# Hybrid encoder step: per-layer embeddings' products from float32 to split operands, in a new place of the queues

## The reference

```
z   = rmsnorm(h) @ w_in                      # split into latents, gates g_a, g_c, convolution input
y_a = rmsnorm(attention * silu(g_a))         # 512 columns, after the attention
y_c = rmsnorm(silu(layernorm(conv)) * silu(g_c))   # 512 columns
h   = h + concat([y_a, y_c]) @ w_out
gate = sigmoid(rmsnorm(h) @ w_pg)
h   = h + gate * (p @ w_pe)                  # p: per-layer input embeddings, 256 wide
```

## Time and profile before

| | us |
|---|---|
| median of three runs | 765.39 |
| the profiled execution's own time | 765.02 |
| its span | 762.9 |
| TensorE busy | 749.0 |
| VectorE busy | 562.0 |
| ScalarE busy | 428.2 |
| GpSimd busy | 91.6 |

### The profile page before, as it was taken

One profiled execution on the slowest core, in us unless ns is written; L12 is line 12 of the kernel. 1 busy time (PEld: TensorE's weight loads), 2 busy tenths in 40 slices (PEclk: granted clock), 3 DMA queues, 4 the chain that ended last, 5 costly groups with the idle time before them and its releaser, 6 DMA issues.

```text
span 762.9 us, 10602 instructions
## 1 busy us (share of the span) xinstructions
PE 749.0 (98%) x3749; PEld 601.8 (79%) x3749; DVE 562.0 (74%) x1084; ACT 428.2 (56%) x996; POOL 91.6 (12%) x161
## 2 busy tenths in 40 slices
PE   9999999999999999999999999999999999999995
PEld 7899887767777588888888988877678767888874
DVE  3459978979877986546453798988888879655577
ACT  3865655665566733263366575647655758223564
POOL 1500323420001400000000020353000000000000
PEclk9999999999999999999999999999999999999998
DMA  8742222410011343412282223233111014332203
GB/s 271 229 128 83 88 73 86 115 36 15 35 35 28 123 167 130 134 56 83 66 279 77 91 76 85 82 81 83 41 36 43 1 54 154 110 125 74 88 5 138
DMA packets 50681, 70.69 MB, mean 93 GB/s; under 512 B 15582, under 2 KB 28154, under 8 KB 50614
## 3 DMA queue, kind: packets, MB, share of 16 engines
q1 hardware_dynamic: 44746, 59.27, 24.6%
q0 software_dynamic: 5824, 10.73, 5.2%
q10 hardware_dynamic: 60, 0.02, 0.0%
HBM read 60.79 MB, written 9.27 MB: 92 GB/s over the span
## 4 chain that ended last, share of the span: by engine, by line
PE 89%; DVE 6%; ACT 2%; DMA 1%; issue 1%; SPq 0%; POOL 0%; ACTq 0%
PE acc L692 20%; PE acc L701 20%; PE acc L698 19%; PE sharedT L616 5%; PE acc L836 5%; PE sharedS L930 4%; PE sharedO L944 4%; PE sharedO L616 2%; PE sharedS L616 2%; DVE VT L1623 2%; PE sharedT L902 1%; PE sharedS L888 1%; PE sharedO L874 1%; PE sharedS L889 1%; PE sharedO L913 1%
## 5 line engine op out<-in xcount | busy, mean ns | idle before, releaser
L692 PE MATMUL acc<-WHI,XHI 128*128 128x512 f32 (+1 forms) x710 | 304.7, 429 | 0.8 <-ACT WHI L1115 0.5
L701 PE MATMUL acc<-WHI,XLO 128*128 128x512 f32 (+1 forms) x710 | 274.7, 387 | 0.0
L698 PE MATMUL acc<-WLO,XHI 128*128 128x512 f32 (+1 forms) x710 | 274.3, 386 | 0.0
L1623 DVE SCALAR_TENSOR_TENSOR VT<-UX,CWT,VT 128x640 f32<-128x640 f32 x240 | 211.5, 883 | 5.0
L692 PEld LDWEIGHTS acc<-WHI,XHI 128*128 128x128 f32 x710 | 133.7, 188 | 29.8 <-issue 6.2
L1553 DVE SCALAR_TENSOR_TENSOR WLO<-WR,GT,WHI 128x512 fp32r<-128x512 f32 (+1 forms) x142 | 98.7, 737 | 78.8 <-ACT WHI L1115 78.6
L698 PEld LDWEIGHTS acc<-WLO,XHI 128*128 128x128 f32 x710 | 133.9, 189 | 27.3 <-issue 6.2
L701 PEld LDWEIGHTS acc<-WHI,XLO 128*128 128x128 f32 x710 | 133.3, 188 | 26.2
L1115 ACT ACTIVATE WHI<-WR,GT 128x512 fp32r<-128x512 f32 (+1 forms) x142 | 93.4, 708 | 85.5 <-PE acc L701 85.3
L1336 ACT ACTIVATE SB<-SB,NBIAS 128x128 f32<-128x128 f32 (+2 forms) x80 | 44.4, 555 | 37.0 <-DVE NBIAS L1682 35.6
L1115 ACT ACTIVATE PT<-sharedT 128x384 f32<-128x384 f32 (+1 forms) x80 | 35.6, 444 | 37.1 <-PE sharedT L616 36.9
(11 more groups left out here) (213 smaller groups left out, 884.4 us busy)
## 6 DMA issues: line engine op xcount, KB each, us to landing
WR<-in_w_in_dram SPq DMA_DIRECT2D x32, 256.0 KB, 3.1
WR<-in_w_in_dram SPq DMA_DIRECT2D x16, 512.0 KB, 3.7
WR<-in_w_out_dram SPq DMA_DIRECT2D x16, 512.0 KB, 3.7
WR<-in_w_pg_dram SPq DMA_DIRECT2D x16, 512.0 KB, 3.5
H<-in_x_prompt_dram SPq DMA_DIRECT2D x16, 256.0 KB, 5.2
WR<-in_w_in_dram SPq DMA_DIRECT2D x8, 416.0 KB, 5.8
residual_spill<-H SPq DMA_DIRECT2D x5, 512.0 KB, 3.4
H<-residual_spill SPq DMA_DIRECT2D x10, 256.0 KB, 3.4
```

The costliest lines, as they stand in the source:

```text
L692: mm(out, hi, w_hi, start=(first and k == 0), stop=False)
L698: mm(out, hi, w_lo, start=False, stop=False)
L701: last = mm(out, lo, w_hi, start=False, stop=(final and k == 1))
L1623: stt(out=out, in0=src, scalar=w, in1=out, op0=ALU.mult, op1=ALU.add).then_inc(conv_done, 1)
```

## The change

The embeddings' products become quanta like all others. Their weight pieces are parts and get split (without a gain column); PTR is copied to XHI (rows 4 and 5, free after gc's third piece) by ScalarE in unit 22, and GpSimd subtracts to make XLO. The block pe1 moves behind oa0. The y tiles are transposed two tiles earlier against the embeddings' products. VectorE starts on y ahead of the convolution's norm, and gates and normalisations of the convolution are dealt out between the residual additions. Three taps move. Numbers of parts behind these rise by one or two throughout.

```diff
-BLOCKS = [... "cv", "pe0", "pe1", "oa0", "oa1", "oc0", "oc1", "pg0", "pg1"]
+BLOCKS = [... "cv", "pe0", "oa0", "pe1", "oa1", "oc0", "oc1", "pg0", "pg1"]
-PARTS = [c for c in CHUNKS if c[1][:2] != "pe"]
+PARTS = CHUNKS
-TAP["turn"] = _take(1)
-for _u, _m in enumerate((2, 1, 0, 4, 1, 1, 4, 2, 1, 2, 0, 2, 1, 1, 4, 2, 1, 2, 0, 2, 1, 1, 4, 1, 0, 1, 1, 3)):
+TAP["turn"] = _take(2)
+for _u, _m in enumerate((1, 1, 1, 3, 1, 1, 4, 2, 1, 2, 0, 2, 1, 1, 4, 2, 1, 2, 0, 2, 1, 1, 4, 1, 1, 1, 1, 2)):
...
# SP, piece(j)
-                    if before in PART:
-                        sp.wait_ge(split_ready, PART[before] + 1)
-                    else:
-                        sp.wait_ge(acc_filled[TILES - 1], BLK[pl, name] + 1)
+                    sp.wait_ge(split_ready, PART[before] + 1)
...
# TensorE
-            copied_wait(pe, (l, "p2"))
-            embed(0, 0)
+            pe.wait_ge(p_low, 2 * (l + 1))
+            quantum("pe0", 0, 0)
             values(UNITS - 1)
-            for t in range(1, TILES):
-                embed(0, t)
-            embed(1, 0)
             for t in range(1, TILES):
-                embed(1, t)
-                turn_ya(t - 1)
+                quantum("pe0", 0, t)
+                if t > 1:
+                    turn_ya(t - 2)
             for c in range(2):
                 for t in range(TILES):
                     copied_wait(pe, (l, ("y", t, 0)))
                     quantum("oa0", c, t)
-                    if (c, t) == (0, 0):
-                        turn_ya(TILES - 1)
+                    if c == 0 and t < 2:
+                        turn_ya(t + 3)
+            for t in range(TILES):
+                quantum("pe1", 0, t)
...
# ScalarE
+            def embeddings_high():
+                part_used(act, PART[l, "gc", 2])
+                for k in range(2):
+                    copy(XHI[:, :, 4 + k, :], PTR[:, k, :].rearrange("p (t e) -> p t e", e=P)).then_inc(p_high, 1)
+                if u == 22:
+                    embeddings_high()
+                if u in (28, 30):
+                    high(first_i + 20 + (u - 28) // 2)
...
             for t in range(TILES):
+                embedding_out(1, t)
+                if t == 0:
+                    high(first_i + 24)
                 if t == 1:
+                    v_tanh_out(4)
             for t in range(TILES):
                 act.wait_ge(yc_ready, TILES * l + t + 1)
                 mean_square(Y[:, t, 512:1024], 20 + t, 512)
+            high(first_i + 25)
...
# VectorE
+                if u >= 30:
+                    low(first_i + u - 10)
...
             sample_heads_out()
-            norm_of_conv()
             head_out(HEADS - 1)
...
             low_half((l, ("y", 0, 0)))
+            norm_of_conv()
+            low_half((l, ("y", 1, 0)))
+            low_half((l, ("y", 2, 0)))
+            norm_of_conv_end()
+            low(first_i + 22)
+            low_half((l, ("y", 3, 0)))
+            normed(0)
+            low_half((l, ("y", 4, 0)))
+            normed(1)
             conv_gate(0)
+            normed(2)
             norm_of_y(0)
+            low(first_i + 23)
             for t in range(TILES):
                 onto_residual("oa0", t)
+                if t in (1, 2):
+                    conv_gate(t)
+                    normed(t + 2)
+            low(first_i + 24)
+            conv_gate(3)
+            conv_gate(4)
+            low(first_i + 25)
             norm_of_y(1)
...
# GpSimd
+            for k in range(2):
+                pool.wait_ge(p_high, 2 * l + k + 1)
+                nc.gpsimd.tensor_tensor(XLO[:, :, 4 + k, :], PTR[:, k, :].rearrange("p (t e) -> p t e", e=P),
+                                        XHI[:, :, 4 + k, :].bitcast(F32), ALU.subtract).then_inc(p_low, 1)
```

More of the change, by code:

```diff
@@ L36 @@
 MAGIC = float(0x5F3759DF)
-BLOCKS = ["u0", "zA", "u1", "ga", "gc", "cv", "pe0", "pe1", "oa0", "oa1", "oc0", "oc1", "pg0", "pg1"]
+BLOCKS = ["u0", "zA", "u1", "ga", "gc", "cv", "pe0", "oa0", "pe1", "oa1", "oc0", "oc1", "pg0", "pg1"]
 BLK = {(l, name): l * len(BLOCKS) + i for l in range(DEPTH) for i, name in enumerate(BLOCKS)}
@@ L311, in build @@
         p_in = sem("p_in")
+        p_high = sem("p_high")
+        p_low = sem("p_low")
         wq_rot = sem("wq_rot")
@@ L431, in first_rows, with first_x @@
             return 2 if name[:2] == "oc" else 0
+        def first_x(name):
+            return 2 if name[:2] == "pe" else first_rows(name)
         def gain_column(i, k):
             l, name, c = PARTS[i]
+            if name[:2] == "pe":
+                return None
             col = G_IN if name in ZCOL else G_OUT if name[0] == "o" else G_PG
@@ L680, in quantum @@
                 for k in ks:
-                    row = 2 * (c + first_rows(name)) + k
+                    row = 2 * (c + first_x(name)) + k
                     hi, lo = XHI[:, t, row, :], XLO[:, t, row, :]
@@ L826, in filler @@
                     quantum(name, c, t, (k,))
[L828 to L839, removed]
             def turn_conv(t):
@@ L1445, in scalar_layer, with ya_square @@
             act.wait_ge(conv_done, CONVS * (l + 1))
[L1446 to L1451, removed]
+            def ya_square(t):
                 act.wait_ge(ya_ready, TILES * l + t + 1)
                 mean_square(Y[:, t, 0:512], 15 + t, 512)
-                if t == 1:
[L1455 to L1463, removed]
+            embedding_out(0, 0)
+            embedding_out(0, 1)
+            ya_square(0)
+            embedding_out(0, 2)
+            high_half((l, ("y", 0, 0)))
+            ya_square(1)
+            embedding_out(0, 3)
+            high_half((l, ("y", 1, 0)))
+            embedding_out(0, 4)
+            high_half((l, ("y", 2, 0)))
+            high(first_i + 22)
+            high_half((l, ("y", 3, 0)))
+            ya_square(2)
+            high_half((l, ("y", 4, 0)))
+            ya_square(3)
+            ya_square(4)
+            v_tanh_out(0)
+            v_tanh_out(1)
+            high(first_i + 23)
+            v_tanh_out(2)
+            v_tanh_out(3)
+            for t in range(TILES):
+                embedding_out(1, t)
+                if t == 0:
+                    high(first_i + 24)
+                if t == 1:
+                    v_tanh_out(4)
             for t in range(TILES):
@@ L1471, in scalar_layer @@
                 if t == 0:
-                    high(first_i + 24)
-            for i in range(25, 28):
+                    high(first_i + 26)
+            for i in range(27, 30):
                 high(first_i + i)
@@ L1857, in vector_layer @@
                 if t == 0:
-                    low(first_i + 24)
+                    low(first_i + 26)
                 if t > 1:
@@ L1862, in vector_layer @@
             onto_residual("oa1", 4)
-            low(first_i + 25)
-            low(first_i + 26)
+            low(first_i + 27)
+            low(first_i + 28)
             for t in range(TILES):
@@ L1867, in vector_layer @@
                 if t == 3:
-                    low(first_i + 27)
+                    low(first_i + 29)
                 if t > 1:
@@ L1872, in vector_layer @@
             low_half((l, ("h", 4, 0)))
-            low(first_i + 28)
+            low(first_i + 30)
             for t in range(TILES):
@@ L1878, in vector_layer @@
                 if t == 1:
-                    low(first_i + 29)
-            low(first_i + 30)
-            low(first_i + 31)
+                    low(first_i + 31)
+            low(first_i + 32)
+            low(first_i + 33)
             dve.wait_ge(squares, SQUARES * l + 30)
@@ L1884, in vector_layer @@
             nc.vector.tensor_scalar(HR[:, 0:5], RS[:, 25:30], 0.5, None, ALU.mult).then_inc(rstd_ready, 1)
-            low(first_i + 32)
+            low(first_i + 34)
             def gate_embedding(half, t):
@@ L1900, in vector_layer @@
             if last:
-                low(first_i + 35)
+                low(first_i + 37)
                 dve.wait_ge(lnf_in, 16)
@@ L1907, in vector_layer @@
             else:
-                low(first_i + 34)
-                low(first_i + 35)
+                low(first_i + 36)
+                low(first_i + 37)
                 gains(l + 1)
@@ L1912, in vector_layer @@
                     low_half((l + 1, ("x", t, 0)))
-                low(first_i + 36)
+                low(first_i + 38)
             def rstd_of_tile(t):
```

45 lines of the change are left out of this document (16 added, 29 removed).

## The result

The changed kernel takes 768.63 us (median of six runs, 767.65 to 770.47). The kernel before took 765.24 beside it (six runs, 764.79 to 766.03). The ratio is 1.0048, with an interval of 1.0036 to 1.006: slower by half a per cent. The profiled execution took 770.33 us, one of the longest, with a span of 768.4.

The account below looks back on a forecast made before the run. The prediction took TensorE's queue, busy 98% of the span, as the bound. Its terms, -3.6 - 1.7 + 5.3 + 1.5, gave +1.5 us a layer, +3.0 in all, hence 768.4 us, with a range of 764.2 to 770.8.

Parts of the forecast that it names:

- A, products: Embeddings' products on TensorE: ten tiles as split products, 1.36 us each in place of 1.72, save 3.6 us a layer.
- B, taps: Convolution taps dealt anew: TensorE's stalls before the scores of units 6 and 30 go, gaining 1.7 us a layer.
- C, hold: Unit 22: GpSimd's two subtractions hold up VectorE's taps, costing 1.5 us a layer (bounds 0 and 2.7).
- D, VectorE late: Behind the units: VectorE can't keep up and TensorE stalls, costing 5.3 us a layer (bounds 4.3 and 6.3).
- the replay: Step-by-step timing of the new order from the first embeddings product: five TensorE stalls, 5.3 us a layer.
- Rival 4: TensorE's clock falls in the new stalls: half speed for 3 us costs 1.5 a layer more, 771.4; chance 0.03.
- Rival 2: VectorE's additions come in time, stalls behind the units halve to 2.7 us, no GpSimd hold: 760.1 us; chance 0.08.

Follow-up runs that it names:

- the new dealing alone: The kernel before with only the new deal of the convolution's taps: 761.44 us, ratio 0.9948.
- the one with zeros: The changed kernel with GpSimd writing zeros into the embeddings' low part in place of subtracting: 766.63 us, ratio 1.0012.
- the late subtraction: The changed kernel with GpSimd's subtraction held until all taps are done: 766.74 us; with VectorE's five oa0 additions in a row as well, 756.95.
- The additions in a row: The changed kernel with VectorE's five oa0 additions in a row and ScalarE's sixth weight part before y's squares: 759.01 us, ratio 0.9921.
- the fastest version: The changed kernel with the late subtraction, y4's low half before the first normalised tile, one gate and normalised tile between additions 2 and 4: 754.60 us.

## Why the prediction was right, and where it was not

The median came out at 768.63 against 768.4 forecast. The direction and the mechanisms of all four terms held, but that the total is so close is partly luck: the terms together were 0.3 us a layer too high, and a rival with a chance of 3 in 100 made up for it. Per layer:

| step | foretold | measured | from |
|---|---|---|---|
| A, products | -3.6 | -3.3 | the stretch, 42.1 to 38.8 |
| B, taps | -1.7 | -1.95 | the new dealing alone, against 765.35 |
| C, hold | +1.5 | +1.35 | changed kernel beside the one with zeros, by product (1.0 by the medians of the late subtraction) |
| D, VectorE late | +5.3 | +5.1 | the stretch, 38.8 to 43.9 |
| clock | 0 | about +0.5 | the rest, 1.0 / 2 |

The first four make +1.2 a layer, so 765.24 + 2.4 = 767.6. One execution has a mean clock (0.996) that speaks for no fall, and it took 767.65. The median leaves 1.0 us for the clock, less than the 1.6 of one fall; the clock's term is a remainder and takes up the errors of the others.

**A and B** hold. A is a little small. The second product behind a group of transposes starts 0.32 us later and not 0.23; there are seven such places in the stretch now and there were two, which covers the 0.3 (an estimate).

**D** is the step that decided the sign, and the replay held place by place: foretold 0.5, 0.4, 1.4, 2.1 and 0.9 us. The brackets and distances of the changed kernel's trace give 0.4, 0.4, 1.3, 2.05 and 0.5 to 0.7, each on the instruction named. The traces of the versions laid side by side, with the clock at 1.00, give 0.5, 0.4, 1.3, 2.1 and 0.8, which is the 5.1 of the stretch; the fifth is shorter in the changed kernel because TensorE comes later there, behind the slow products. The additions in a row give back the last three. It follows from one thing in the diff: two pairs of gate and normalised tile, 2.8 us each, stand between additions that TensorE now asks for every 1.36 us.

**Rival 4**, the clock, happened. It got 3 in 100 because no stand of the kernel before was long enough to show what follows one, and I took the longest single stand (2.1 us) as the measure. The rows show that two stands close together count as well. The price was right: 1.5 us a fall foretold, 1.6 measured. The additions in a row, without these stands, had a clock of 1.00 and a difference to the changed kernel of 4.8 us a layer, more than the last three places of D. Rival 2 (stalls of half the length) is refuted by the waits.

## What to carry to other kernels

When a block changes place and hands its accumulators on to another, the engine that frees them becomes a producer with a deadline: write down when TensorE asks for each tile and put no more between the ones that free them than the deadline leaves room for. The same change gains 10.6 us in the fastest version. As written it lost 3.4, mostly because four instructions of 0.7 us stood twice in the wrong place, and partly because a subtraction ran beside the taps and the clock fell. Look at the granted clock of the few microseconds behind a stand before taking the stand as the whole loss, and move work of GpSimd that reads SBUF to where VectorE does not read two operands, or where its delay costs nothing.

## What the runs showed of the hardware that I had not expected

- Behind stands of 1.2 and 1.95 us with 1.5 us of products between them, in most executions but not all, the granted clock went to 1.2 GHz for about 3.4 us; the first products behind the stand still ran at 2.4 GHz (276.16 and 276.39 start 0.23 apart). The same program thus has runs 3 us apart.
- GpSimd's subtraction of 128x640 took 1.54 us undisturbed. Beside VectorE's two-operand taps the two engines took turns by whole instructions: taps of 0.88 us took 1.91 and 2.06, and the second subtraction 2.12, so VectorE lost 2.2 us and GpSimd 0.6. A copy with one operand read (0.72 us undisturbed) did the same on a smaller scale, 0.5 us for two; a memset (0.63) cost the taps nothing.
